# Prompt attention: both score halves of a head ahead of both masks, maxima and exponentials

## The reference, cut to what matters

```
scale = HEAD_DIM ** -0.5
mask = (start + jnp.arange(Q_BLOCK))[:, None] >= key_pos[None, :]
p1 = masked_softmax(jnp.einsum('bqhd,bkhd->bhqk', q1, k1).astype(jnp.float32) * scale, mask)
p2 = masked_softmax(jnp.einsum('bqhd,bkhd->bhqk', q2, k2).astype(jnp.float32) * scale, mask)
p = (p1 - lam * p2).astype(v.dtype)
return jnp.einsum('bhqk,bkhe->bqhe', p, v)
```

## Time and profile before

| what | us |
|---|---|
| median of 3 runs | 1470.77 |
| lowest and highest run | 1462.28, 1472.52 |
| span of the profiled execution | 1465.0 |
| prompt attention in it, first scores to last values | 799 to 970 |
| PE busy in the span | 1253.8 |
| DVE busy in the span | 916.1 |
| ACT busy in the span | 698.6 |

### The profile page before, as it was taken

The page is one execution under the profiler, slowest core; times in us unless marked ns, Lnnn a source line. Parts: engine busy times, 40 slices in busy tenths (PEclk is TensorE's granted clock), DMA queues, the critical chain, the costliest instruction groups (busy, mean ns, idle before and its releaser), DMA issues.

```text
span 1465.0 us, 16900 instructions
## 1 busy us (share of the span) xinstructions
PE 1253.8 (86%) x5888; PEld 963.9 (66%) x5888; DVE 916.1 (63%) x1112; ACT 698.6 (48%) x748; POOL 252.7 (17%) x261
## 2 busy tenths in 40 slices
PE   5989994599999996299999999989937999999930
PEld 4766764478888885277776666657736788888820
DVE  4256357498888885832321444464675988888836
ACT  4233223277777775222112544432224777777721
POOL 2021020241111121410000000000302411112314
PEclk9999995699999998599999999969858999999975
DMA  9302047269999996732230133213462899999842
GB/s 341 122 29 93 1 173 285 84 224 359 374 372 372 376 368 214 296 116 92 89 116 1 59 116 115 78 48 118 187 238 83 302 376 373 369 375 371 299 181 77
DMA packets 142529, 302.56 MB, mean 207 GB/s; under 512 B 11888, under 2 KB 12048, under 8 KB 142352
## 3 DMA queue, kind: packets, MB, share of 16 engines
q1 hardware_dynamic: 123024, 250.23, 47.9%
q0 software_dynamic: 19168, 51.31, 9.8%
q10 hardware_dynamic: 288, 0.36, 0.1%
HBM read 288.36 MB, written 30.28 MB: 217 GB/s over the span
## 4 chain that ended last, share of the span: by engine, by line
PE 78%; DVE 13%; DMA 3%; ACT 3%; issue 2%; POOLq 0%; POOL 0%; SPq 0%; DVEq 0%; ACTq 0%
PE ps L1422 20%; PE ps L1424 20%; PE ps L1423 20%; PE ps L1657 3%; DVE wl L868 2%; PE ps L1720 2%; PE ps L1705 2%; PE ps L1581 2%; DVE x L1225 2%; PE ps L1467 2%; ACT wh L617 2%; PE ps L1674 1%; PE ps L1691 1%; DMA xg<-x_rows,gcur 1%; DMA yl<-y_rows 1%
## 5 line engine op out<-in xcount | busy, mean ns | idle before, releaser
L868 DVE TENSOR_TENSOR wl<-raw,wh 128x2048 fp32r<-128x2048 f32 x210 | 481.0, 2314 | 221.3 <-ACT wh L617 217.4
L617 ACT ACTIVATE wh<-raw 128x2048 fp32r<-128x2048 f32 x210 | 398.4, 1915 | 202.0 <-PE ps L1424 138.0
L1422 PE MATMUL ps<-wh,xTh 128*128 128x512 f32 (+1 forms) x560 | 227.7, 407 | 22.8 <-DVE wl L868 14.8
L1424 PE MATMUL ps<-wh,xTl 128*128 128x512 f32 (+1 forms) x560 | 223.0, 398 | 0.0
L1423 PE MATMUL ps<-wl,xTh 128*128 128x512 f32 (+1 forms) x560 | 223.0, 398 | 0.0
L1422 PE MATMUL ps<-wh,xgTh 128*128 128x512 f32 x512 | 209.3, 409 | 6.7 <-DVE xgTl L1175 5.7
L1423 PE MATMUL ps<-wl,xgTh 128*128 128x512 f32 x512 | 203.9, 398 | 0.0
L1424 PE MATMUL ps<-wh,xgTl 128*128 128x512 f32 x512 | 203.5, 398 | 0.0
L1422 PEld LDWEIGHTS ps<-wh,xTh 128*128 128x128 f32 (+1 forms) x560 | 98.6, 176 | 58.9 <-issue 22.5
L1422 PEld LDWEIGHTS ps<-wh,xgTh 128*128 128x128 f32 x512 | 97.3, 190 | 36.2 <-DVE wl L868 8.3
L1424 PEld LDWEIGHTS ps<-wh,xTl 128*128 128x128 f32 (+1 forms) x560 | 98.0, 175 | 34.2
(11 more groups left out here) (258 smaller groups left out, 1641.1 us busy)
## 6 DMA issues: line engine op xcount, KB each, us to landing
raw<-in_moe_w_up SPq DMA_DIRECT2D x120, 1024.0 KB, 10.5
raw<-in_moe_w_down SPq DMA_DIRECT2D x62, 1024.0 KB, 11.7
raw<-in_a_w_in SPq DMA_DIRECT2D x8, 1024.0 KB, 16.7
ahead_up<-in_moe_w_up SPq DMA_DIRECT2D x8, 1024.0 KB, 8.7
yl<-y_rows POOLq DMA_DIRECT2D x8, 1024.0 KB, 8.4
raw<-in_cache_k SPq DMA_DIRECT2D x16, 512.0 KB, 3.8
raw<-in_cache_v SPq DMA_DIRECT2D x16, 512.0 KB, 4.9
raw<-in_a_w_out SPq DMA_DIRECT2D x4, 1024.0 KB, 5.1
```

Of the source, the lines that this page charges most:

```text
L617: act.activation(wh[:, slot], src, ACT.Copy).then_inc(high[key], 1)
L868: dve.tensor_tensor(wl[:, slot], src, wh[:, slot].bitcast(F32), ALU.subtract).then_inc(low[key], 1)
L1422: pe.matmul(out, high_, w_high, start=start, stop=False)
L1424: return pe.matmul(out, low_, w_high, start=False, stop=stop)
```

## The change

On TensorE both halves' score matmuls stand next to each other at the head of the step, then both masks; they wait for the second exponential of the step before (`at_exp` at 2n), where each half waited for its own. On DVE both maxima stand ahead of P of step n-1. On ACT both exponentials stand ahead of the output copy, the key copy and the copy of the transposed P. No instruction is added or taken away. The whole diff:

```
@@ -815,6 +815,7 @@
                 if n < steps:
                     att_exp(n, 0)
+                    att_exp(n, 1)
                 if n >= 2:
                     att_o(n - 2)
                 if n < steps and j < 4:
@@ -822,7 +823,6 @@
                 if 1 <= n <= steps:
                     att_pt(n - 1)
                 if n < steps:
-                    att_exp(n, 1)
                     if j < 4:
                         keys_copy(g, 2 * j + 1)
@@ -1350,10 +1350,9 @@
                 if n < steps:
                     att_max(n, 0)
+                    att_max(n, 1)
                 if n:
                     att_p(n - 1)
-                if n < steps:
-                    att_max(n, 1)
                 if n == steps:
                     break
@@ -1648,16 +1647,18 @@
-            def scores(n, part):
+            def scores(n):
                 qt, h = att_step(n)
                 w = (qt + 1) * P
-                r = slice(64 * part, 64 * part + 64)
-                after(pe, at_exp, 2 * (n - 1) + part + 1)
-                pe.matmul(ps[:, part, 0:w], QT[r, h, qt * P:(qt + 1) * P], KT[r, h, 0:w], start=True, stop=False,
-                          skip_group_check=True)
-                pe.matmul(ps[:, part, w - P:w], idmask[:, 0], idmask[:, 1], start=False, stop=True,
-                          skip_group_check=True).then_inc(at_s, 1)
+                after(pe, at_exp, 2 * n)
+                for part in range(2):
+                    r = slice(64 * part, 64 * part + 64)
+                    pe.matmul(ps[:, part, 0:w], QT[r, h, qt * P:(qt + 1) * P], KT[r, h, 0:w], start=True, stop=False,
+                              skip_group_check=True)
+                for part in range(2):
+                    pe.matmul(ps[:, part, w - P:w], idmask[:, 0], idmask[:, 1], start=False, stop=True,
+                              skip_group_check=True).then_inc(at_s, 1)
@@ -1734,7 +1735,7 @@
                 if n < steps:
-                    scores(n, 0)
+                    scores(n)
                 if n >= 2:
                     values(n - 2)
@@ -1744,7 +1745,6 @@
                     if 1 <= j < 5 and g:
                         sample_values(g - 1, (j - 1) // 2, (j - 1) % 2)
-                    scores(n, 1)
                 if 1 <= n <= steps:
                     turn_p(n - 1)
```

## The result

The changed kernel takes 1460.49 us (median of 10 runs, 1455.77 to 1461.59) against 1471.45 of before (10 runs): a ratio of 0.9929, 95% interval 0.9911 to 0.9948. It is faster by 0.7%, where 0.3% slower was forecast, and 1460.5 lies just under the forecast range.

What follows compares the result with a forecast made beforehand. Prompt attention looked TensorE-bound, with the scores-maximum-P-transposes chain pacing some steps. Covered steps -5.9, the other steps +12.5 in sum, step 31 -2.0: +4.6 us on 1470.8, forecast 1475.4, range 1461 to 1494.

Steps and rivals of the forecast that it cites:

- d: TensorE, time from the start of a step's pair of score matmuls to the mask; forecast 3x + 0.32, 0.64 to 1.60 us.
- x: TensorE, length of one score matmul, priced at 0.107 us per 128 columns.
- the lower of the two ends: TensorE, both halves' scores run side by side: 2x + 0.21, what one half takes now.
- The upper end: TensorE, the halves' scores one after the other: 4x + 0.32, giving 1484 us; chance 0.20, with falls up to 1498.
- The chain of two maxima and P: DVE, both maxima precede P of step n-1, so its transposes start 2.00 to 2.39 us after the first mask.
- the covered steps: Attention, j = 1 to 4 of groups 1 to 3, 12 steps: stay TensorE-bound and gain 5.9 us together.
- the rival's d: TensorE, halves side by side, d = 2x + 0.21: -8 us in all, 1463, or 1468 with a fall; chance 0.17.
- I carry the difference over: Whole kernel: the median's 5.8 us above the profiled span is kept, so 1470.8 + 4.6 = 1475.4 us.
- The rival on the clock: Attention, new holes in steps 5 to 7 lower TensorE's clock one to three times: 1480 to 1491 us; chance 0.18.
- The price of a fall: TensorE, each fall of the granted clock costs about 5 us, with up to three more falls.
- the two signs: Prediction is wrong if steps 0 to 7 don't lengthen, or if the granted clock falls inside the stage.
- The last step: Attention's end, step 31 from scores to transposes of its own P: 9.0 us becomes 7.0, gaining 2.0.

Runs made afterwards that it cites:

- the kernel with the same ones: Changed kernel with both score matmuls of a head read from partitions 0 to 63, second half's scores left out: 1482.61 us, ratio 1.0069 to before.
- the first profiles: The first profiled executions of the kernel before (span 1465.0 us, attention 167.0) and of the changed kernel (attention 161.0); no further edit.
- the second profile: The kernel before, unedited, run and profiled again: median 1471.61 us, span 1469.9, attention 173.0 in place of 167.0.
- the other chip: The changed kernel, unedited, run again on another chip beside kernels with parts of it undone: 1460.15 us, ratio 0.9922 to before.
- the two better orders: Changed kernel with P of step n-1 ahead of both maxima on DVE: 1453.88 us; also with the first key copy between both exponentials on ACT: 1447.93.
- DVE undone: Changed kernel with DVE's old order (first maximum, P of step n-1, second maximum): 1468.76 us, ratio 0.9976 to before.
- ACT undone: Changed kernel with ACT's old order (second exponential behind the copy of the transposed P): 1476.22 us, ratio 1.0044 to before.

## Why the prediction was wrong, point by point

The step that failed is the choice of d in the part on TensorE, "three lengths of x stand in a row, d = 3x + 0.32 ... I take this one: partitions differ, order is kept". The pair measures 0.64, 0.85 and 1.06 us at 256, 384 and 512 columns, which is 2x + 0.21, the lower of the two ends that the text gave. The argument from the queue's order doesn't hold: the second half's first matmul starts within 0.02 us of the first half's first, although the code issues the whole of the first half ahead of it. That each engine runs what is written in the order in which it is written, as the part on the kernel before has it, is thus not borne out by the starts of these four; how the two instructions of one f32 matmul are queued, the trace does not tell. The rule of the Trainium skill that stood beside the sum, "TensorE: Matmul & The Clock Gate", Part 3 (Packing small matmuls), said that they overlap. By that rule, taken fully, the result was 1463; the traces agree with the overlap, and with its condition of different rows, by the kernel with the same ones. That starts keep program order, which the rule says too, they do not bear out for the four instructions, unless those are queued in another order than the code's. The upper end was off a little: 1.48 us at 384 is 4x + 0.21, not 4x + 0.32.

With the right d the rest of the sum holds. For step 5 it gives 5.9 - 0.43 = 5.47, measured 5.40; for step 6 3.55 - 0.32 = 3.23, measured 3.23; step 7 3.9 - 0.43 = 3.47, measured 3.46; step 21 6.28 - 0.54 = 5.74, measured 5.64. The chain of two maxima and P, the holes on TensorE and where they stand came as forecast; the covered steps gained 9.7 us, by the rival's d 12 x 0.86 = 10.3. The rival's whole was -8, measured -6.0 between the first profiles. That its 1463 lies only 2.5 us from the measured time is in part luck: the first profiles show 2 us less than its gain, and 5 of the 11 between the medians are not in them at all.

A second step failed that no case held: "I carry the difference over". Of the 5.8 us some 1.8 lie outside the span (1471.71 and 1469.9 in the second profile); most of the rest is that the profiled execution of before was not like its median: its attention ran in a quicker form, 167 us where the one near the median takes 173. The rival on the clock looked at holes in the kernel after and took those of before as given. In the second profile, before already pays for the hole at 911 to 913 with 20 us at the lower clock; both profiles of the changed kernel pay 3 to 4 us for a fall at the same place (915 to 918, and 913 to 917 on the other chip).

The price of a fall was too high for the changed kernel: it does fall more often (809 to 813, 915 to 918, 956 to 959), but each stretch lasts 3 to 4 us. Step 23 took 4.57 us, 0.9 more than 1.06 + 2.39 + 0.15 + 0.11 = 3.71 gives; 5 us a fall were forecast. A fall inside the stage was one of the two signs that the prediction gave for being wrong, and it came; the other did not, steps 0 to 7 did lengthen.

The last step gained 2.9 us where 2.0 were forecast, in part because d was shorter and in part because its clock differed.

## What to carry to other kernels

Two matmuls with 64 rows each cost the time of one here when they read different partitions and nothing stood between them in TensorE's queue; a mask of full height between them cost the whole gain, so look for pairs of heads or halves that can be issued together. Then read again which chain ends last: here the pair emptied TensorE, and the order on DVE and ACT decided another 12 us. That a full TensorE had hidden them is likely, but no run tried the two better orders with the halves apart. Where a kernel's runs lie in clusters, take a second profile before you carry a sum over to their median.

## What the runs showed of the hardware that was not expected

How long a fall of the granted clock lasts differs widely between the kernels: 3 to 4 us in the changed kernel, 20 us in the second profile of before though TensorE shows 2.0 of 2.0 us busy in its windows, 10 to 14 us in the kernel with masks between the halves and in the one with equal rows. Falls that begin in the last step and run on past it left aside, the long ones are all in kernels whose halves don't overlap but for two (804 to 819 with DVE undone, 834 to 845 with ACT undone), where TensorE also waited inside the stretch. That the overlap shortens them fits, but no run changed only that at the same waits, so the cause stays open. And the same hole, with the same instructions around it, let the clock pass in one execution of before and lowered it in another. Timeline of the first profile, then of the second (the transposes of P in step 22, four instructions; 0.66 us is the full clock, 1.11 the lower one):

```profile
913.34 0.66 PE L1666 MATMUL ps<-con,Pm 128*128 128x128 f32 x4 [1.17 <-DVE Pm L1291]
```

```profile
913.07 1.11 PE L1666 MATMUL ps<-con,Pm 128*128 128x128 f32 x4 [1.17 <-DVE Pm L1291]
```
